# Nine chunk places in rotation for the expert weights, and VectorE's 32x32 turns in a triangular inversion

## The chip, the core and the metric

The kernel runs on one core of a Trainium2 chip. The metric is the time of the whole program on the device, in microseconds; lower is better. The profile gives the span from the first to the last instruction, which is a little shorter than that time. TensorE (PE in the profile) multiplies matrices, VectorE (DVE) and ScalarE (ACT) work on elements, and SyncE (SP) issues nearly all of the loads. "PEld" is the load of the stationary operand of a matmul.

## The reference, cut to what matters

A decoder block over 256 tokens of width 1024, in f32. It has three stages.

1. A mixer. Half of its heads are attention, the other half a gated delta rule over chunks of 64 tokens. For four heads and four chunks the delta rule solves a lower triangular system whose diagonal is one:

```
a_strict = where(strict, (k_beta @ k.T) * decay, 0)             # 64 x 64 for each head and chunk
uw = triangular_solve(a_strict + I, rhs, lower, unit_diagonal)  # rhs: v * beta | k_beta * exp(g)
```

2. Cross attention over 256 memory tokens.
3. A mixture of 32 experts, four for each token. Each expert has a gate and up matrix (1024 x 2048), a clamped SwiGLU and a down matrix (1024 x 1024). Whatever the routing is, the kernel reads all 32 experts' weights: 32 x 12 MiB.

## The kernel before

**Queues and buffers.** Each engine runs its own instruction list, and semaphores order them. Weights come in chunks of 128 x 4096 f32, 2 MiB, each a contiguous piece of its matrix. `ring` has six such places (`slot(0)` to `slot(5)`). `W_ORDER` names the 13 chunks of the first two stages; the n-th goes to slot n mod 6. SP issues one DMA for a chunk (L350, for experts L382) after it has waited for `slot_free`, which TensorE raises when the place's last matmul is done. TensorE waits for `slot_loaded`.

**The experts.** They are taken in 16 pairs with `PAIR_CHUNKS` = 12 chunks each: 0 to 3 are gate and up of the pair's first expert, 4 to 7 those of the second, 8 and 9 the first down matrix, 10 and 11 the second. `gate_up` (L1558) and `down` (L1585) are the matmuls that read chunks, `gather` (L1537) picks the tokens of the two experts of the next pair, and L1623 adds a pair's result to the tokens. Three more places lie in the `work` buffer (`extra`, numbers 6, 7 and 8), where data of the earlier stages is dead by then. For the first pair alone, chunks 6, 7 and 8 go into these; they are loaded in the order 0, 1, 2, 3, 6, 4, 7, 8, 5, 9, 10, 11. Place 6 may be written once ScalarE has the biases ready (`biases_ready`), places 7 and 8 after ScalarE has drained `x_pv1`, a step near the end of cross attention. All other chunks go round the six slots, `chunk_place` says where. TensorE and SP run pair 0 as straight code and the pairs 1 to 14 (SP: 1 to 15) in a loop with one pair in its body. Further passes over all experts exist for the case that one expert has more than 64 tokens; they are not entered with these inputs.

**The inversion.** The 64 x 64 systems are kept as eight matrices of 128 x 128, each with two systems on its diagonal. The inverse is built in six levels, each of which joins diagonal blocks two by two: `a_mat` masked to the level's blocks is `level_l` (`level_part`, L786 on VectorE). With the inverse so far as `inv` and its transpose as `inv_T`, a level is: `swap`n = level_l.T inv_T (TensorE, eight matmuls, L1244), ScalarE copies it out (L447), `solve_T`n = inv.T swap, which VectorE subtracts from inv_T (L890), and `solve`n, the same product the other way round, which VectorE subtracts from inv (L894). Level 0 needs no product: `inv` = 1 - level_l (L806), and `swap0` turns level_l on TensorE (against the identity), from which VectorE makes inv_T (L879). The blocks of `inv` are 2 wide after level 0 and 32 wide after level 4; level 5 makes inv_T alone.

**The order around it.** `EARLY`, `MIDDLE` and `LATE` are lists written by hand. In `MIDDLE` the levels stand between quarters of projections, such as `moba_v.0` (16 matmul records of 128 x 256, L1296 or L1300), so that TensorE has work while the others copy. Every named step writes one of four pairs of PSUM banks, and `take` waits until the pair's last content has been drained. Quarters use pair 3, the levels the pairs 0 and 1 in turn.

Of the kernel before, what the change touches and what calls it, by code (L numbers as in the profile page):

```python
# [20 lines left out]
ALU = mybir.AluOpType  # L21
# [20 lines left out]
PAIR_CHUNKS = 12  # L42
EPS = 1e-6
# [18 lines left out]
MIDDLE = ["swap0", "moba_v.0", "swap1", "moba_v.1", "solve_T1", "solve1", "moba_v.2", "swap2", "moba_v.3", "solve_T2",  # L62
# [34 lines left out]
def bass_hybrid_block(nc, x, mem, norm_mix_g, w_in, gdn_conv_w, gdn_A_log, gdn_dt_bias, gdn_norm_g,  # L97
                      moba_norm_g, w_out, norm_xattn_g, norm_mem_g, xattn_w_q, xattn_w_kv, xattn_w_o,
                      norm_ffn_g, router_w, router_b, w_gate_up, b_gate_up, w_down, b_down, final_norm_g, out):
    with ExitStack() as ctx:  # L100
# [196 lines left out]

        def slot(s):
            return ring[:, s * SLOT:(s + 1) * SLOT]
# [27 lines left out]
        def _(sp):  # L327
# [33 lines left out]
            def load_pair(i, before, first=False):  # L361


                gu = [w_gate_up[0, bass.ds(2 * i + k, 1)].rearrange("e (c p j) n -> p (e c) (j n)", p=P, j=2)
                      for k in range(2)]
                dn = [w_down[0, bass.ds(2 * i + k, 1)].rearrange("e (c p j) n -> p (e c) (j n)", p=P, j=4)
                      for k in range(2)]

                for c in (0, 1, 2, 3, 6, 4, 7, 8, 5, 9, 10, 11) if first else range(PAIR_CHUNKS):
                    dst, loaded, free, use = chunk_place(c, first)  # L370
                    if c < 8:
                        src = gu[c // 4][:, c % 4, :]
                    else:
                        src = dn[(c - 8) // 2][:, c % 2, :]
                    if free:
                        sp.wait_ge(S(free), 2 * before + use)
                    else:

                        sp.wait_ge(S("biases_ready"), 1)
                        if c > min(extra):  # L380
                            drained(sp, "x_pv1")
                    sp.dma_start(dst, src).then_inc(S(loaded), 16)  # L382

            load_pair(0, 0, first=True)
            with sp.Fori(1, PAIRS) as i:
                load_pair(i, i)
# [3 lines left out]
            with sp.If(most > SLOTS):  # L390
                with sp.Fori(1, PASSES) as r:
                    with sp.If(most > r * SLOTS):
                        with sp.Fori(0, PAIRS) as i:
                            load_pair(i, sp.snap(r * PAIRS + i))
# [41 lines left out]
        def _(act):  # L436
# [76 lines left out]
            for name in MIDDLE:  # L513
# [6 lines left out]
                elif name.startswith("swap") and name != "swap0":  # L520
# [124 lines left out]
        def _(v):  # L645
# [160 lines left out]
            nc.vector.tensor_tensor(inv, eye, level_l, ALU.subtract).then_inc(S("solved"), 1)  # L806
            drained(v, "tok_v")
# [372 lines left out]
        def _(pe):  # L1180
# [162 lines left out]
            for name in MIDDLE:  # L1343
# [201 lines left out]
            def chunk_landed(c, before, first):  # L1545
                place, loaded, free, use = chunk_place(c, first)
                pe.wait_ge(S(loaded), 32 * before + 16 * (use + 1))
                return place, free

            def gate_up(k, before, first):  # L1550
                for c in range(4):
                    place, free = chunk_landed(4 * k + c, before, first)
                    w = place.rearrange("p (k n) -> p k n", n=2 * D_MODEL)
# [6 lines left out]
                    if free:  # L1560
                        last.then_inc(S(free), 1)
# [13 lines left out]
            def down(k, n, before, first):  # L1575
# [4 lines left out]
                for c in range(2):  # L1580
                    place, free = chunk_landed(8 + 2 * k + c, before, first)
                    w = place.rearrange("p (k n) -> p k n", n=D_MODEL)
# [5 lines left out]
                    if free:  # L1588
                        last.then_inc(S(free), 1)
# [5 lines left out]
            def pair_of_experts(r, i, before, n, m, first=False, final=False):  # L1595
# [5 lines left out]
                gate_up(0, before, first)  # L1601
# [9 lines left out]
                gate_up(1, before, first)  # L1611
# [3 lines left out]
                down(0, n, before, first)  # L1615
                act_turned(1, m)
                down(1, m, before, first)
# [14 lines left out]
            def expert_pass(r, first=False):  # L1632
                pe.wait_ge(S("picked"), PAIRS * r + 1)
                gather(0, 0)
                gather(1, 0)
                drained(pe, "count")
                pe.wait_ge(S("count_ready"), 1)
                pe.wait_ge(S("biases_ready"), 1)
                if first:
                    pair_of_experts(r, 0, 0, 1, 2, first=True)  # L1640
                with pe.Fori(1 if first else 0, PAIRS - 1) as i:
                    pair_of_experts(r, i, pe.snap(r * PAIRS + i), pe.snap(r * E + 2 * i + 1),
                                    pe.snap(r * E + 2 * i + 2))
                i = PAIRS - 1
                pair_of_experts(r, i, pe.snap(r * PAIRS + i), pe.snap(r * E + 2 * i + 1), pe.snap(r * E + 2 * i + 2),
                                final=True)
# [3 lines left out]
            expert_pass(0, first=True)  # L1650
            most = pe.value_load(count_i[0:1, 0:1], min_val=0, max_val=SEQ)
            with pe.If(most > SLOTS):
                with pe.Fori(1, PASSES) as r:
                    with pe.If(most > r * SLOTS):
                        expert_pass(r)
# [24 lines left out]
```

## Time and profile before

| | us |
|---|---|
| median of three runs | 1262.95 (1260.44 to 1263.8) |
| the profiled execution, its own time | 1259.65 |
| its span | 1257.9 |
| TensorE busy with matmuls | 1127.2 (90%) |
| VectorE busy | 362.6 (29%) |
| ScalarE busy | 160.1 (13%) |
| bytes moved by DMA | 435.43 MB, 346 GB/s over the span |

How to read it: TensorE's share is that of a pipelined engine and counts records one after the other, so 90% doesn't say that it sets the end. The span falls into the two first stages (0 to about 324 us) and the experts (from there to 1239 us), with a short end. These two have to be read apart, in windows, together with the DMA rate.

### The profile page before, as it was taken

How to read it: one execution, taken by the hardware profiler on the slowest of the kernel's cores; microseconds unless marked ns; L12 is line 12 of the kernel's file. 1: busy time of each engine (PE TensorE's matmuls, PEld its weight loads, DVE VectorE, ACT ScalarE, POOL GpSimd, SP SyncE). 2: the span in 40 equal slices, each digit the busy share in tenths (PEclk: the TensorE clock that was granted, in tenths of full speed). 3: DMA queues.
4: the chain of work that ended last, by engine and by line, in shares of the span. 5: the costliest groups of instructions: out<-in, count | busy, mean ns of one | idle time of the engine just before them, and what ended most of it. 6: DMA issues, size and time to landing. Idle time of an engine off the chain costs nothing.

```text
span 1257.9 us, 15864 instructions
## 1 busy us (share of the span) xinstructions
PE 1127.2 (90%) x6688; PEld 556.9 (44%) x6688; DVE 362.6 (29%) x713; ACT 160.1 (13%) x241; POOL 5.5 (0%) x23
## 2 busy tenths in 40 slices
PE   7999998888899999898989898999989898989895
PEld 6889987475433333332423333333323232333331
DVE  5582234244321321221221312212122121221312
ACT  3431133243000000100000000000010000000001
POOL 1000000000000000000000000000000000000000
PEclk9999998998899999999999999999999999999998
DMA  9731221465588999999999999999999999999994
GB/s 336 268 134 68 67 68 67 110 261 207 219 356 359 427 429 427 429 429 428 429 427 429 429 428 429 427 430 428 428 429 427 430 428 428 430 427 430 428 428 188
DMA packets 45159, 435.43 MB, mean 346 GB/s; under 512 B 6581, under 2 KB 6666, under 8 KB 20458
## 3 DMA queue, kind: packets, MB, share of 16 engines
q1 hardware_dynamic: 42986, 433.16, 82.6%
q10 hardware_dynamic: 2144, 1.86, 0.7%
q8 instruction: 22, 0.36, 0.1%
q14 instruction: 7, 0.06, 0.0%
HBM read 433.95 MB, written 1.05 MB: 346 GB/s over the span
## 4 chain that ended last, share of the span: by engine, by line
PE 64%; DMA 27%; DVE 5%; ACT 2%; issue 1%; SPq 0%; ACTq 0%; DVEq 0%
PE ps L1558 28%; DMA ring<-in_w_down 25%; PE ps L1585 7%; PE ps L1623 5%; PE ps L1244 4%; PE ps L1200 4%; PE ps L1537 4%; PE ps L1300 3%; PE ps L1296 2%; PE ps L1182 2%; DVE work L1125 2%; PE ps L1429 1%; PE ps L1473 1%; DMA work<-in_b_down 1%; DMA ring<-in_w_in 1%
## 5 line engine op out<-in xcount | busy, mean ns | idle before, releaser
L1558 PE MATMUL ps<-ring,work 128*64 128x512 f32 x2016 | 445.4, 595 | 22.3 <-DMA ring<-in_w_gate_up 20.8
L1558 PEld LDWEIGHTS ps<-ring,work 128*64 128x64 f32 x2016 | 141.9, 137 | 302.2 <-issue 258.9
L1585 PE MATMUL ps<-ring,work 128*64 128x512 f32 x1008 | 229.1, 598 | 42.5 <-ACT work L623 23.6
L1585 PEld LDWEIGHTS ps<-ring,work 128*64 128x64 f32 x1008 | 68.3, 136 | 181.6 <-issue 113.4
L1102 DVE TENSOR_SCALAR work<-ps 128x512 f32<-128x512 f32 x32 | 21.9, 686 | 212.9 <-PE ps L1182 212.9
L621 ACT ACTIVATE work<-work 128x512 f32<-128x512 f32 x32 | 20.2, 630 | 488.7 <-DVE work L1102 488.7
L1125 DVE COPY work<-ps 128x1024 f32<-128x1024 f32 x16 | 19.6, 1224 | 217.6 <-PE ps L1591 217.6
L1623 PE MATMUL ps<-work 128*128 128x512 f32 x128 | 59.2, 605 | 21.1 <-DVE work L1125 21.1
L1117 DVE COPY work<-ps 128x512 f32<-128x512 f32 x16 | 11.1, 691 | 229.8 <-PE ps L1182 229.8
L1182 PE MATMUL ps<-small,work 128*128 128x128 f32 (+1 forms) x353 | 57.6, 297 | 13.6 <-DMA work<-in_gdn_conv_w 6.4
L623 ACT COPY work<-ps 128x512 f32<-128x512 f32 x32 | 18.7, 585 | 363.1 <-PE ps L1182 363.1
L1244 PE MATMUL ps<-work 128*128 128x128 f32 (+4 forms) x440 | 58.9, 286 | 6.1 <-ACT work L519 2.8
L1182 PEld LDWEIGHTS ps<-small,work 128*128 128x128 f32 (+1 forms) x353 | 44.2, 170 | 41.6 <-issue 39.8
L1200 PE MATMUL ps<-work,ring 128*128 128x256 f32 x256 | 58.7, 388 | 2.6 <-DMA ring<-in_w_in 2.2
L1244 PEld LDWEIGHTS ps<-work 128*128 128x128 f32 (+2 forms) x440 | 54.0, 187 | 11.4 <-issue 4.8
L1537 PEld LDWEIGHTS ps<-work 128*128 128x128 bf16 x1536 | 49.2, 100 | 10.9 <-issue 8.6
L1200 PEld LDWEIGHTS ps<-work,ring 128*128 128x128 f32 x256 | 49.1, 195 | 10.0 <-issue 3.4
L1537 PE MATMUL ps<-work 128*128 128x64 bf16 x1536 | 49.7, 196 | 2.3 <-DVE work L1065 2.3
L1130 DVE TENSOR_TENSOR work<-work,ps 128x1024 f32<-128x1024 f32 x32 | 39.1, 1221 | 42.3 <-PE ps L1623 42.3
L1623 PEld LDWEIGHTS ps<-work 128*128 128x128 f32 x128 | 23.0, 189 | 55.2 <-DVE work L1125 32.3
L1300 PE MATMUL ps<-ring,work 128*128 128x256 f32 x192 | 46.0, 395 | 0.0
L1300 PEld LDWEIGHTS ps<-ring,work 128*128 128x128 f32 x192 | 37.1, 198 | 5.7 <-issue 0.3
(209 smaller groups left out, 665.6 us busy)
## 6 DMA issues: line engine op xcount, KB each, us to landing
ring<-in_w_gate_up SPq DMA_DIRECT2D x126, 2048.0 KB, 24.8
ring<-in_w_down SPq DMA_DIRECT2D x63, 2048.0 KB, 22.9
ring<-in_w_in SPq DMA_DIRECT2D x7, 2048.0 KB, 16.0
ring<-in_xattn_w_kv SPq DMA_DIRECT2D x2, 2048.0 KB, 14.5
ring<-in_w_out SPq DMA_DIRECT2D x2, 2048.0 KB, 8.4
work<-in_w_gate_up SPq DMA_DIRECT2D x2, 2048.0 KB, 12.8
ring<-in_xattn_w_q SPq DMA_DIRECT2D x1, 2048.0 KB, 9.4
ring<-in_xattn_w_o SPq DMA_DIRECT2D x1, 2048.0 KB, 8.9
```

What stands on the lines that cost most here:

```text
L1102: nc.vector.tensor_scalar(gate_sb, bank(GATE_BANK[k]), LIMIT, None, ALU.min) \
L1125: nc.vector.tensor_copy(y_sb, ps[:, 512 * Y_BANK:512 * Y_BANK + 1024].rearrange("p (a b) -> p a b", b=512)).then_inc(S("y_ready"), 1)
L1130: nc.vector.tensor_tensor(x_sb[:, t, :], x_sb[:, t, :], ps[:, 512 * b:512 * b + 1024], ALU.add).then_inc(S("combined"), 1)
L1182: return nc.tensor.transpose(dst, src, ident[0:n_in, 0:n_in])
L1200: last = nc.tensor.matmul(pair(name)[:, SEQ * b:SEQ * b + SEQ], w[:, k, b * P:(b + 1) * P], moving[:, k, :], start=(k == 0), stop=(k == KB ...
L1244: return nc.tensor.matmul(dst, still, moving, start=True, stop=True)
L1296: last = nc.tensor.matmul(pair(name)[:, SEQ * q:SEQ * q + SEQ], w[:, k, q * P:(q + 1) * P], hT[:, k, :], start=(k == 0), stop=(k == KB - 1))
L1300: last = nc.tensor.matmul(halves(name)[:, t, c:c + 256], tokens[:, k, t * P:(t + 1) * P], w[:, k, c:c + 256], start=(k == 0), stop=(k == K ...
L1537: last = nc.tensor.matmul(dst[:, SLOTS * b:SLOTS * b + SLOTS], split[s][:, t, 2 * P * (b // 2) + b % 2:2 * P * (b // 2 + 1):2], pick[k][:, ...
L1558: last = nc.tensor.matmul(bank(b)[p], xg_T[k][:, kb, :], w[:, kk, 512 * q:512 * q + 512], start=(kb == 0), stop=False)
L1585: last = nc.tensor.matmul(bank(Y_BANK + y)[p], act_T[:, b, HALF * c:HALF * c + HALF], w[:, b, 512 * q:512 * q + 512], start=(c == 0 and b ...
L1623: last = nc.tensor.matmul(bank(b + q), g_T[:, q, P * t:P * t + P], y_sb[:, q, :], start=True, stop=True)
```

## The change

Two parts. First, the expert chunks of the first pass go round nine places, the six slots and the three in `work`, in the order `PLACES`, instead of six. 36 chunks, three pairs, are four turns of the nine places, so the loops of TensorE and SP now have three pairs in their body (four turns, pairs 1 to 12); pair 0 and the pairs 13 to 15 are straight code. The chunks are loaded in their order, 0 to 11. The first load of each place in `work` waits for both `biases_ready` and `x_pv1`.

Second, the turns in the inversion. `inv_T` of level 0 and `inv` after the levels 1 to 4 are made by VectorE with `transpose`, which turns each 32 x 32 block in its own place; since the blocks of these matrices are at most 32 wide, that is their transpose. `swap0` and `solve1` to `solve4` are gone, on TensorE and VectorE. `level_part(1)` comes before `tok_v` is scaled.

```diff
+PLACES = [1, 2, 3, 4, 5, 6, 7, 8, 0]
+TURN_PAIRS = 3
+TURN_USES = TURN_PAIRS * PAIR_CHUNKS // len(PLACES)
+TURNS = (PAIRS - 1 - TURN_PAIRS) // TURN_PAIRS
...
-MIDDLE = ["swap0", "moba_v.0", "swap1", "moba_v.1", "solve_T1", "solve1", "moba_v.2", "swap2", "moba_v.3", "solve_T2",
-          "solve2", "moba_q.0", "swap3", "moba_q.1", "solve_T3", "solve3", "moba_q.2", "swap4", "moba_q.3",
-          "solve_T4", "solve4", "moba_k.0", "moba_k.1", "swap5", "moba_k.2", "solve_T5", "moba_k.3", "u",
+MIDDLE = ["moba_v.0", "swap1", "moba_v.1", "solve_T1", "moba_v.2", "swap2", "moba_v.3", "solve_T2",
+          "moba_q.0", "swap3", "moba_q.1", "solve_T3", "moba_q.2", "swap4", "moba_q.3",
+          "solve_T4", "moba_k.0", "moba_k.1", "swap5", "moba_k.2", "solve_T5", "moba_k.3", "u",
           "w_T", "score0", "state0", "gdn_z.0", "v1", "inter1", "probs_T0", "state1", "gdn_z.1", "pv0",
...
-        FIRST_RING = PAIR_CHUNKS - len(extra)
-
-        def chunk_place(c, first):
-            if first and c in extra:
-                return extra[c], f"extra_loaded{c}", None, 0
-            if first:
-                n = PRE + c - sum(e < c for e in extra)
-            else:
-                n = PRE + FIRST_RING + c - PAIR_CHUNKS
-            return slot(n % RING), f"slot_loaded{n % RING}", f"slot_free{n % RING}", n // RING
+        def place(s):
+            return slot(s) if s < RING else extra[s]
+
+        def uses_before_experts(s):
+            return len(range(s, PRE, RING)) if s < RING else 0
+
+        def first_pass_chunk(i, c):
+
+            g = PAIR_CHUNKS * i + c
+            s = PLACES[g % len(PLACES)]
+            return s, uses_before_experts(s) + g // len(PLACES)
+
+        def later_pass_chunk(c):
+
+            s = c % RING
+            return s, uses_before_experts(s) + len(range(PLACES.index(s), PAIRS * PAIR_CHUNKS, len(PLACES))) + c // RING
...
-                for c in (0, 1, 2, 3, 6, 4, 7, 8, 5, 9, 10, 11) if first else range(PAIR_CHUNKS):
-                    dst, loaded, free, use = chunk_place(c, first)
+                for c in range(PAIR_CHUNKS):
+                    s, use = chunk(c)
                     if c < 8:
                         src = gu[c // 4][:, c % 4, :]
                     else:
                         src = dn[(c - 8) // 2][:, c % 2, :]
-                    if free:
-                        sp.wait_ge(S(free), 2 * before + use)
+                    if s >= RING and use == 0:
+
+                        sp.wait_ge(S("biases_ready"), 1)
+                        drained(sp, "x_pv1")
                     else:
-
-                        sp.wait_ge(S("biases_ready"), 1)
-                        if c > min(extra):
-                            drained(sp, "x_pv1")
-                    sp.dma_start(dst, src).then_inc(S(loaded), 16)
-
-            load_pair(0, 0, first=True)
-            with sp.Fori(1, PAIRS) as i:
-                load_pair(i, i)
+                        sp.wait_ge(S(f"slot_free{s}"), turned + use)
+                    dst = place(s)
+                    sp.dma_start(dst, src).then_inc(S(f"slot_loaded{s}"), 16)
+
+            load_pair(0, lambda c: first_pass_chunk(0, c), 0)
+            with sp.Fori(0, TURNS) as rev:
+                turned = sp.snap(rev * TURN_USES)
+                for q in range(1, TURN_PAIRS + 1):
+                    load_pair(rev * TURN_PAIRS + q, lambda c: first_pass_chunk(q, c), turned)
+            for i in range(PAIRS - TURN_PAIRS, PAIRS):
+                load_pair(i, lambda c: first_pass_chunk(i, c), 0)
...
             nc.vector.tensor_tensor(inv, eye, level_l, ALU.subtract).then_inc(S("solved"), 1)
+            v.wait_ge(S("solved"), 1)
+            nc.vector.transpose(flat(inv_T), flat(inv)).then_inc(S("inv_T_begun"), 1)
+            level_part(1)
             drained(v, "tok_v")
             nc.vector.tensor_tensor(tok_v, tok_v, spread(beta, P), ALU.mult).then_inc(S("vb_ready"), 1)
...
-                if name == "swap0":
-                    filled(v, name)
-                    drain_done(nc.vector.tensor_tensor(inv_T, eye, blocks(name), ALU.subtract), name)
-                    v.wait_ge(S("solved"), 1)
-                    level_part(1)
-                    drained(v, name)
-                elif name.startswith("swap"):
+                if name.startswith("swap"):
 
                     if n + 1 < LEVELS:
                         filled(v, name)
                         level_part(n + 1)
                 elif name.startswith("solve_T"):
                     filled(v, name)
+                    if n == 1:
+                        v.wait_ge(S("inv_T_begun"), 1)
                     drain_done(nc.vector.tensor_tensor(inv_T, inv_T, blocks(name), ALU.subtract), name)
                     drained(v, name)
-                elif name.startswith("solve"):
-                    filled(v, name)
-                    drain_done(nc.vector.tensor_tensor(inv, inv, blocks(name), ALU.subtract), name)
-                    drained(v, name)
+                    if n + 1 < LEVELS:
+                        nc.vector.transpose(flat(inv), flat(inv_T)).then_inc(S("inv_turned"), 1)
...
-                elif name == "swap0":
-                    pe.wait_ge(S("level_ready"), 1)
-                    eight(name, lambda b, dst: mm(dst, level_l[:, b, :], ident))
                 elif name.startswith("swap"):
                     pe.wait_ge(S("level_ready"), n + 1)
-                    drained(pe, "swap0" if n == 1 else f"solve_T{n - 1}")
+                    if n == 1:
+                        pe.wait_ge(S("inv_T_begun"), 1)
+                    else:
+                        drained(pe, f"solve_T{n - 1}")
                     eight(name, lambda b, dst: mm(dst, level_l[:, b, :], inv_T[:, b, :]))
                 elif name.startswith("solve_T"):
                     drained(pe, f"swap{n}")
                     if n == 1:
                         pe.wait_ge(S("solved"), 1)
                     else:
-                        drained(pe, f"solve{n - 1}")
+                        pe.wait_ge(S("inv_turned"), n - 1)
                     eight(name, lambda b, dst: mm(dst, inv[:, b, :], swap[:, b, :]))
-                elif name.startswith("solve"):
-                    eight(name, lambda b, dst: mm(dst, swap[:, b, :], inv[:, b, :]))
...
-            def chunk_landed(c, before, first):
-                place, loaded, free, use = chunk_place(c, first)
-                pe.wait_ge(S(loaded), 32 * before + 16 * (use + 1))
-                return place, free
-
-            def gate_up(k, before, first):
+            def chunk_landed(s, use, turned16):
+                pe.wait_ge(S(f"slot_loaded{s}"), turned16 + 16 * (use + 1))
+                return place(s)
+
+            def gate_up(k, chunk, turned16):
                 for c in range(4):
-                    place, free = chunk_landed(4 * k + c, before, first)
-                    w = place.rearrange("p (k n) -> p k n", n=2 * D_MODEL)
+                    s, use = chunk(4 * k + c)
+                    w = chunk_landed(s, use, turned16).rearrange("p (k n) -> p k n", n=2 * D_MODEL)
...
+            def first_pass():
+                begin_pass(0)
                 drained(pe, "count")
                 pe.wait_ge(S("count_ready"), 1)
                 pe.wait_ge(S("biases_ready"), 1)
-                if first:
-                    pair_of_experts(r, 0, 0, 1, 2, first=True)
-                with pe.Fori(1 if first else 0, PAIRS - 1) as i:
+                pair_of_experts(0, 0, 0, 1, 2, lambda c: first_pass_chunk(0, c), 0)
+                with pe.Fori(0, TURNS) as rev:
+                    turned16 = pe.snap(rev * (16 * TURN_USES))
+                    for q in range(1, TURN_PAIRS + 1):
+                        i = pe.snap(rev * TURN_PAIRS + q)
+                        pair_of_experts(0, i, i, pe.snap(2 * i + 1), pe.snap(2 * i + 2),
+                                        lambda c: first_pass_chunk(q, c), turned16)
+                for i in range(PAIRS - TURN_PAIRS, PAIRS):
+                    pair_of_experts(0, i, i, 2 * i + 1, 2 * i + 2, lambda c: first_pass_chunk(i, c), 0,
+                                    final=(i == PAIRS - 1))
```

## Rows read from the trace of the kernel before

**Rows 1.** The page: busy time of the engines, and GB/s in 40 equal slices.
```profile
PE 1127.2 (90%) x6688; PEld 556.9 (44%) x6688; DVE 362.6 (29%) x713; ACT 160.1 (13%) x241; POOL 5.5 (0%) x23
...
GB/s 336 268 134 68 67 68 67 110 261 207 219 356 359 427 429 427 429 429 428 429 427 429 429 428 429 427 430 428 428 429 427 430 428 428 430 427 430 428 428 188
```

**Rows 2.** Windows of one pair each; the last two columns are DMA share and GB/s.
```profile
651.19:709.91 58.72, 52.64 (x320) 19.85 (x321) 13.37 (x27) 3.71 (x5) 0.00 (x0) 1.00 1.01 428
324.26:379.00 54.74, 52.02 (x322) 20.48 (x321) 13.82 (x30) 3.71 (x5) 0.00 (x0) 0.99 0.84 343
```

**Rows 3.** Chain that ended last: last down chunk of pair 3 and of pair 14.
```profile
533.73 3.65 PE ps L1585 x16
...
1179.74 3.65 PE ps L1585 x16
```

**Rows 4.** Timeline of the end: the last down chunk and the last instruction.
```profile
1238.80 3.65 PE L1585 MATMUL ps<-ring,work 128*64 128x512 f32 x16 [1.23 <-DMA ring<-in_w_down]
...
1253.55 1.28 DVE L1176 SCALAR_TENSOR_TENSOR work<-work,small 128x1024 f32<-128x1024 f32 x1
```

**Rows 5.** SP's own timeline, the issues of chunks around the start of the experts.
```profile
294.30 0.33 SPq L382 DMA_DIRECT2D work<-in_w_gate_up  x1
...
303.18 0.33 SPq L382 DMA_DIRECT2D ring<-in_w_gate_up  x1
...
328.23 0.33 SPq L382 DMA_DIRECT2D ring<-in_w_down  x1
...
346.70 0.33 SPq L382 DMA_DIRECT2D ring<-in_w_gate_up  x1
...
362.48 0.33 SPq L382 DMA_DIRECT2D ring<-in_w_gate_up  x1
...
382.82 0.33 SPq L382 DMA_DIRECT2D ring<-in_w_gate_up  x1
```

**Rows 6.** Windows of 5 us: the stream's start and the two dips of its rate.
```profile
330.00:335.00 5.00, 5.00 (x26) 1.65 (x24) 0.00 (x0) 0.00 (x0) 0.00 (x0) 1.00 0.94 380
...
360.00:365.00 5.00, 4.32 (x24) 1.85 (x22) 0.00 (x0) 1.73 (x2) 0.00 (x0) 1.00 0.37 85
...
380.00:385.00 5.00, 5.00 (x26) 1.69 (x24) 0.00 (x0) 0.00 (x0) 0.00 (x0) 1.00 0.31 69
```

**Rows 7.** TensorE's timeline of pair 0 and the start of pair 1.
```profile
324.26 14.23 PE L1558 MATMUL ps<-ring,work 128*64 128x512 f32 x64
...
363.89 7.09 PE L1585 MATMUL ps<-ring,work 128*64 128x512 f32 x32 [0.68 <-ACT work L623]
...
379.00 13.95 PE L1558 MATMUL ps<-ring,work 128*64 128x512 f32 x64
```

**Rows 8.** Timeline of the inversion's head and its first full level.
```profile
87.34 1.95 PE L1244 MATMUL ps<-small,work 128*128 128x128 f32 x16
87.54 1.01 ACT L447 COPY work<-ps 128x1024 f32<-128x1024 f32 x1 [0.36 <-PE ps L1182]
...
88.94 1.23 DVE L806 TENSOR_TENSOR work<-small,work 128x1024 f32<-128x1024 f32 x1
...
92.35 1.22 DVE L786 TENSOR_TENSOR work<-work,small 128x1024 f32<-128x1024 f32 x1
...
93.62 2.05 PE L1244 MATMUL ps<-work 128*128 128x128 f32 x16 [0.88 <-DVE work L786]
...
95.51 3.62 PE L1300 MATMUL ps<-ring,work 128*128 128x256 f32 x16
...
98.96 3.73 PE L1244 MATMUL ps<-work 128*128 128x128 f32 x32
```

**Rows 9.** VectorE by line and shape: one input of 1024 columns; two of 2048.
```profile
L662 DVE TENSOR_SCALAR work<-work,small 128x1024 f32<-128x1024 f32 x6 | 4.5, 753 | 0.2
...
L767 DVE TENSOR_TENSOR work<-work 128x2048 f32<-128x2048 f32 x1 | 2.3, 2292 | 0.0
```

**Rows 10.** DMA queues, an instruction queue: packets, MB, share of 16 engines.
```profile
q8 instruction: 22, 0.36, 0.1%
```

More of the change, by code:

```diff
@@ L296, in spread, with flat @@
             return v.unsqueeze(2).to_broadcast([v.shape[0], v.shape[1], n])
+        def flat(v):
+            return v.rearrange("p a b -> p (a b)")
         def slot(s):
@@ L359, in _, with load_pair @@
                             .then_inc(S(f"mem_loaded{t}"), 16)
-            def load_pair(i, before, first=False):
+            def load_pair(i, chunk, turned):
                 gu = [w_gate_up[0, bass.ds(2 * i + k, 1)].rearrange("e (c p j) n -> p (e c) (j n)", p=P, j=2)
@@ L393, in _ @@
                         with sp.Fori(0, PAIRS) as i:
-                            load_pair(i, sp.snap(r * PAIRS + i))
+                            load_pair(i, later_pass_chunk, sp.snap((r - 1) * 2 * PAIRS + 2 * i))
             for t in range(TILES):
@@ L519, in _ @@
                     drain_done(nc.scalar.copy(m_pT, halves(name)[:, :, 0:384]), name)
-                elif name.startswith("swap") and name != "swap0":
+                elif name.startswith("swap"):
                     evacuate(name, swap, blocks(name))
@@ L1559, in gate_up @@
                                                     start=(kb == 0), stop=False)
-                    if free:
-                        last.then_inc(S(free), 1)
+                    last.then_inc(S(f"slot_free{s}"), 1)
                 for q, (b, p) in enumerate(((GATE_BANK[k], low), (GATE_BANK[k], high),
@@ L1573, in act_turned, with down @@
                 last.then_inc(S("act_T_filled"), 1)
-            def down(k, n, before, first):
+            def down(k, n, chunk, turned16):
                 pe.wait_ge(S("act_T_ready"), n)
@@ L1580, in down @@
                 for c in range(2):
-                    place, free = chunk_landed(8 + 2 * k + c, before, first)
-                    w = place.rearrange("p (k n) -> p k n", n=D_MODEL)
+                    s, use = chunk(8 + 2 * k + c)
+                    w = chunk_landed(s, use, turned16).rearrange("p (k n) -> p k n", n=D_MODEL)
                     for b in range(4):
@@ L1587, in down @@
                                                     start=(c == 0 and b == 0), stop=False)
-                    if free:
-                        last.then_inc(S(free), 1)
+                    last.then_inc(S(f"slot_free{s}"), 1)
                 for q, (y, p) in enumerate(places):
@@ L1593, in down, with pair_of_experts @@
                 last.then_inc(S("down_filled"), 1)
-            def pair_of_experts(r, i, before, n, m, first=False, final=False):
+            def pair_of_experts(r, i, before, n, m, chunk, turned16, final=False):
                 pe.wait_ge(S("gathered"), E * r + 2 * i + 1)
@@ L1600, in pair_of_experts @@
                 pe.wait_ge(S("combined"), 2 * before + 1)
-                gate_up(0, before, first)
+                gate_up(0, chunk, turned16)
                 pe.wait_ge(S("gated_picked"), PAIRS * r + i + 1)
@@ L1610, in pair_of_experts @@
                 pe.wait_ge(S("gathered"), E * r + 2 * i + 2)
-                gate_up(1, before, first)
+                gate_up(1, chunk, turned16)
                 act_turned(0, n)
                 pe.wait_ge(S("gated_T_ready"), before + 1)
-                down(0, n, before, first)
+                down(0, n, chunk, turned16)
                 act_turned(1, m)
-                down(1, m, before, first)
+                down(1, m, chunk, turned16)
                 pe.wait_ge(S("y_ready"), before + 2)
@@ L1630, in pair_of_experts, with begin_pass @@
                     gather(1, 0)
-            def expert_pass(r, first=False):
+            def begin_pass(r):
                 pe.wait_ge(S("picked"), PAIRS * r + 1)
@@ L1638, in expert_pass, with later_pass @@
                 pe.wait_ge(S("biases_ready"), 1)
-                if first:
-                    pair_of_experts(r, 0, 0, 1, 2, first=True)
-                with pe.Fori(1 if first else 0, PAIRS - 1) as i:
+                pair_of_experts(0, 0, 0, 1, 2, lambda c: first_pass_chunk(0, c), 0)
[8 more added lines that the diff above has]
+                                    final=(i == PAIRS - 1))
+            def later_pass(r):
+                begin_pass(r)
+                done = pe.snap((r - 1) * PAIRS)
+                with pe.Fori(0, PAIRS - 1) as i:
                     pair_of_experts(r, i, pe.snap(r * PAIRS + i), pe.snap(r * E + 2 * i + 1),
-                                    pe.snap(r * E + 2 * i + 2))
+                                    pe.snap(r * E + 2 * i + 2), later_pass_chunk, pe.snap(done * 32 + 32 * i))
                 i = PAIRS - 1
                 pair_of_experts(r, i, pe.snap(r * PAIRS + i), pe.snap(r * E + 2 * i + 1), pe.snap(r * E + 2 * i + 2),
-                                final=True)
+                                later_pass_chunk, pe.snap(done * 32 + 32 * i), final=True)
             pe.sem_inc(S("act_T_filled"), 1)
-            expert_pass(0, first=True)
+            first_pass()
             most = pe.value_load(count_i[0:1, 0:1], min_val=0, max_val=SEQ)
@@ L1654, in _ @@
                     with pe.If(most > r * SLOTS):
-                        expert_pass(r)
+                        later_pass(r)
 _INS = ["x", "mem", "norm_mix_g", "w_in", "gdn_conv_w", "gdn_A_log", "gdn_dt_bias", "gdn_norm_g", "moba_norm_g",
```

## The prediction

> **What bounds the kernel now.** I read the page's slices first. From slice 14 (409 us) on the loads run at 427 to 430 GB/s without a break, while in the slices before they move less [rows 1]. So there are two regimes. The windows of one pair say what each costs: a late pair takes 58.72 us at a DMA share of 1.01; pair 0, for which nine chunks lay ready, takes 54.74 us [rows 2]. TensorE alone would need 54.74 us for a pair, the loads need 58.72 us, 4.893 us for each of 12 chunks. The chain shows how exact this is: from the last down chunk of pair 3 to that of pair 14 it is 646.01 us, 11 pairs of 58.73 us [rows 3]. The last chunk of all is multiplied at 1238.80 us, at once after its landing, and 19.1 us of adding, norm and store follow to the end of the span, 1257.9 us [rows 4]. Nothing that TensorE does after 500 us sets the end. It is: the time at which the stream of 183 chunks (192 less the nine loaded ahead) begins, plus 183 x 4.893 = 895.4 us, plus what the stream idles, plus the tail.
>
> **Where the stream begins and idles.** With nine places full, SP waits for TensorE's first chunk: the experts' matmuls begin at 324.26 us [rows 7] and SP issues the tenth chunk at 328.23 us [rows 5]. The reader is to see in the next issues that only six slots come round. Six chunks go out up to 346.70 us; the next is issued at 362.48 us, since it waits for slot 1, which holds chunk 9, a down chunk of pair 0. While TensorE works on the chunks in places 6, 7 and 8 it frees nothing. Three issues follow from 362.48 us on, then again none until 382.82 us, when the first chunk of pair 1 is done [rows 5]. The windows over these stretches show 85 and 69 GB/s [rows 6].
>
> I rebuild it as a queue: a chunk starts 1.76 us after its issue if the queue is empty (from the 380 GB/s of the window up to 335 us [rows 6]), else behind the one ahead, and takes 4.893 us. The stream starts at 329.99 us. Six chunks are done at 359.35, the seventh starts at 364.24: 4.9 us idle. The eighth starts 0.35 us late, the ninth ends at 379.27 and the tenth starts at 384.58: 5.3 us idle. Together 10.5 us. Check: 329.99 + 895.4 + 10.5 = 1235.9 us; TensorE takes the last chunk at 1238.80, so 2.9 us lie between end of service and use. I keep these as they are.
>
> **Part one, nine places.** Chunk 9 now goes to the place of chunk 0, and every later one nine behind. The frees of pair 0, counted from its matmul rows [rows 7], come at 327.9, 331.3, 334.8, 338.2, 343.0, 346.4, 349.9, 353.4, 358.7, 362.1, 367.4 and 370.9 us, the next at 382.5 us with pair 1. Twelve chunks keep the queue busy until 329.99 + 12 x 4.893 = 388.7 us, and the thirteenth can start at 384.6 (its issue at 382.82 us and 1.76). That is the tightest place, with 4.1 us in hand; each later pair adds 58.72 - 54.74 = 4.0 us. So the 10.5 us go to zero: **-10.5 us**. After that the nine places give nothing, as six already keep the stream full.
>
> The loading order also moves. Chunks 5, 6 and 7 now wait for `x_pv1`, before that chunk 6 did not, and chunk 8 stands behind them on SP. In the clock of before: three issues at 294.30 and one at 303.18 us [rows 5], four chunks in a row, done at 296.1 + 4 x 4.893 = 315.6 us. TensorE starts at 324.26 and wants chunk 5 only at 343. Cost nothing; were the cover gone, one chunk, 4.9 us.
>
> In the steady state SP has about eight chunks out instead of five. No row shows that a longer queue changes the rate: nothing for it.
>
> **Part two, the turns.** Through the levels TensorE has no idle time but 0.9 us; the levels and the quarters follow each other without a gap, so a removed matmul is time. A block of eight is 16 records, 1.95 us alone; `solve_T1` and `solve1` together are 32 records, 3.73 us [rows 8]. Each of `solve1` to `solve4` gives 1.78 us: 7.1 us. VectorE does a turn in place of the subtraction L894. The turn must be done before the next `solve_T`, which comes a quarter (3.62), a swap (1.95) and another quarter later [rows 8]; with the subtraction (1.22 us) ahead of it, some 5 us are in hand. ScalarE's copy of `swap`n lies under a quarter as before.
>
> At the head less is gained. Without `swap0` (87.34 us), `moba_v.0` waits until ScalarE has copied `tok_v` (87.54 + 1.01 us) and starts at 88.7 instead of 89.1; it would be done at 92.2. `swap1` waits for `level_part(1)`, before at 92.35 us, followed by the matmul at 93.62 [rows 8]. Now VectorE does L806 at 88.94, the turn from 90.20 and `level_part(1)` after it; scaling `tok_v` is behind these. The trace has no such turn. Its cost for 128 x 1024 f32 is bounded by the nearest rows: 0.75 us for one input from SBUF at the same size, 2.29 us for two inputs of twice the size [rows 9]. I take 1.22, as nearly all rows of 1024 columns have [rows 8]. Then `level_part(1)` ends at 92.56 and `swap1` starts at 92.6: **-1.0 us**; with the bounds -1.4 and 0. This is the only place where the turn's length counts.
>
> The Trainium skill (VectorE: DVE Perf Modes, section The three transpose paths) gives 311 ns for a turn of 128 x 128 bf16; eight of these would be 2.5 us, an estimate from that page, and by it the head would gain nothing and the sum come out 1.0 us higher. No row here shows a turn.
>
> So the front is shorter by 8.1 us. Does that arrive at 324 us? After the levels everything is released by TensorE, VectorE or ScalarE, or by loads that SP and ScalarE issue after one of them; nothing in the chain there is tied to a fixed time. **-8.1 us**, bounds 7.1 and 8.5. The stream then starts 8.1 us earlier.
>
> **Part three, what the loops cost.** A pair is 320 + 321 records on TensorE [rows 2]. Four more bodies are now straight code (one body before and one in the loop, now four and three). An instruction queue moved 0.36 MB in 22 packets, 16.4 KB each [rows 10]; 2 x 6688 records of TensorE [rows 1] less 13 repeated pairs of 641 are 5043, so 71 bytes for each record, waits included. A loop's body fetched once fits these numbers; fetched each time there would be 0.59 MB more. Four more bodies are 0.18 MB, 11 packets: at 429 GB/s 0.4 us of the stream. I take **+0.5 us**. If one DMA engine carried them all, at 0.9 us for each (0.1% of 16 spans over 22 packets) it would be 10 us. Against that: the straight last pair, three packets, took from 1179.74 to 1238.80, only 0.3 us more than the 58.73 of the others [rows 3, 4].
>
> **Sum.** 1257.9 - 10.5 - 8.1 + 0.5 = 1239.8 us of span. The profiled execution's own time lies 1.75 us above its span: 1241.5. The median of the runs shown is 3.3 us above that execution, so I forecast 1244.5 us. What a measurement of this kernel can't tell from no change is about 0.3%, 4 us.
>
> **The rivals.**
> (a) Both parts pay as above: 1244.5 us, own range 1239 to 1250 (turn at its bounds, gap 9 to 11.5 us, up to 5 us of code loads). Chance 0.74.
> (b) Only the queue pays; the front's 8 us are lost to a wait behind it. For: the front has many waits of VectorE and ScalarE. Against: the chain there holds only short ones. 1252.6 us. Chance 0.07.
> (c) Only the front pays: the stream still idles, because SP's order or a late release of a place keeps it from using nine. For: each wait on SP holds all loads behind it. Against: the counted frees. 1255.0 us. Chance 0.07.
> (d) Slower: TensorE's loop body no longer stays loaded and is fetched each turn. That body is 3 x 641 records or 137 KB, while rows show only 46 KB held. Three repeats and the four more bodies are 36 packets; on one DMA engine 36 x 0.9 = 33 us that every chunk waits for, so 1277 us with the gains taken off. It decides from 20 packets on; spread over the engines it is 1.4 us and nothing. As stalls of TensorE alone it is hidden: to be the bound, TensorE would have to lose 1223.9 (end of the last chunk then) - 1184.2 (316.2 + 15 pairs of 54.74 + 46.9 for the last, as pair 0 [rows 7]) = 40 us first. Chance 0.08. The Trainium skill (Runtime: NRT & Kernel Launch, section Instruction fetch mechanics) says that a taken branch out of the fetched window forces a load of the target before execution goes on; by that rule the stall exists, and the trace of before shows no such stall at its loop's end.
> (e) No gain within 0.3%, both parts failing: 0.04.
>
> The range reaches over (a), (b) and (c): 1238 to 1255. Faster 0.90, same 0.03, slower 0.07.
>
> **What the profile after would show.** The first expert matmul at 316 us; SP's issues following the frees without the holes of 16 and 12 us; windows of 5 us from 325 to 375 us at 425 GB/s or more; the slices full from slice 11 on; TensorE at 54.7 us for a pair until pair 4 or 5 and at 58.7 us after it; issue to landing of a gate chunk near 39 us instead of 25; the last down chunk at 1220 us; 16 records in place of 32 in four levels, and turns of about 1.2 us. I am wrong if pairs take more than 58.7 us (code loads, or a longer queue slows the stream), if the instruction queue shows 60 packets or more, or if the experts start later than 318 us.

## The result and the profile after

The changed kernel takes 1250.87 us (median of 5 runs, 1246.79 to 1252.57), the kernel before 1261.31 us in the same comparison: ratio 0.991, 95% interval 0.9886 to 0.9936. It is faster by 10.4 us where 18 were forecast. The time lies inside the forecast's range (1238 to 1255), but 0.9 us outside the likeliest case's own range (1239 to 1250). The profiled execution took 1252.57 us, its span is 1250.8 us.

The page of the kernel after, its GB/s in 40 slices and its instruction queue, against [rows 1] and [rows 10]:

```profile
GB/s 338 270 80 122 70 74 61 110 202 268 269 427 426 428 429 427 428 422 428 427 427 428 425 428 427 427 427 428 424 427 427 428 429 427 427 428 429 428 427 125
...
q8 instruction: 61, 1.00, 0.3%
```

Two things are to be seen. The stream is full from slice 11 on, where before it was full from slice 13 on: the holes are closed. And the instruction queue moved 61 packets instead of 22; the prediction had named 60 or more as a sign against it. Its two other signs came too: the experts start at 319.08 us, later than 318, and some pairs take more than 58.7 us. The last down chunk starts at 1231.64 us, not at 1220, and a gate chunk lands 34 to 35 us after its issue (medians of the page), not 39.

SP's timeline and the chain of waits of the kernel after, against [rows 5] and [rows 3]: the first refill, the loop's first jump back, and the last down chunks of pairs 6, 8, 9 and 11:

```profile
322.88 7.20 SPq L394 DMA_DIRECT2D ring<-in_w_down  x3
```

```profile
537.82 6.74 issue
544.55 15.65 PE ps L1568 x64
...
698.37 3.65 PE ps L1594 x16
...
817.37 3.65 PE ps L1594 x16
...
876.10 3.65 PE ps L1594 x16
...
995.10 3.65 PE ps L1594 x16
```

At the end of pair 3, TensorE stands still for 6.7 us with nothing to wait for, and its next 64 records take 15.65 us instead of 13.95 (why is said in the last section). Pair 9, with no turn's end in it, takes 58.73 us as before; pairs 7 and 8 take 119.00 us together and 10 and 11 again 119.00, where two pairs took 117.46 before. Windows of the kernel after, columns as in [rows 2]: pair 0, the standstill, pair 9, and pairs 7 and 8:

```profile
319.15:373.66 54.51, 51.80 (x323) 20.45 (x322) 13.75 (x30) 3.71 (x5) 0.00 (x0) 1.00 0.92 386
...
538.00:545.00 7.00, 0.45 (x2) 0.30 (x4) 0.00 (x0) 0.00 (x0) 0.00 (x0) 0.73 1.02 414
817.37:876.10 58.73, 52.57 (x320) 19.72 (x320) 13.36 (x27) 3.72 (x5) 0.00 (x0) 1.00 1.01 428
698.37:817.37 119.00, 106.35 (x640) 41.57 (x640) 26.74 (x54) 7.43 (x10) 0.00 (x0) 0.97 1.01 427
```

The loads go on during the standstill (414 GB/s), so it isn't waited for by itself; over the turn of pairs 7 to 9 the stream still loses 119.00 - 117.46 = 1.5 us. The end, timeline of TensorE, against [rows 4]:

```profile
1231.64 3.65 PE L1594 MATMUL ps<-ring,work 128*64 128x512 f32 x16 [1.03 <-DMA ring<-in_w_down]
```

The last down chunk still waits for its load and starts at 1231.64 us. From the experts' first matmul (319.08 us) to it are 912.56 us; before they were 1238.80 - 324.26 = 914.54. Of the 10.5 us of holes only 2.0 arrive. I call this length the stream's length below; it doesn't depend on when the front ends.

The head of the inversion, a timeline of all engines after, against [rows 8]:

```profile
93.41 3.72 PE L1313 MATMUL ps<-ring,work 128*128 128x256 f32 x16 [1.10 <-ACT work L463]
93.75 1.23 DVE L822 TENSOR_TENSOR work<-small,work 128x1024 f32<-128x1024 f32 x1
95.00 1.25 DVE L824 STREAM_TRANSPOSE work<-work 128x1024 f32<-128x1024 f32 x1
96.17 1.18 DVE L802 TENSOR_TENSOR work<-work,small 128x1024 f32<-128x1024 f32 x1
...
97.41 2.05 PE L1257 MATMUL ps<-work 128*128 128x128 f32 x16 [0.28 <-DVE work L802]
```

The turn takes 1.25 us (1.22 taken), `moba_v.0` waits 1.1 us for ScalarE's copy of `tok_v`, and `swap1` waits 0.28 us for `level_part(1)`. It all stands 4.8 us later than in the profile before, which has its cause ahead of the change: the first 64 records of a projection took 17.10 us here and 14.05 before. The repetition below shows that it is no part of the change.

### The profile page after: what moved, and what is told of

Its sections match the earlier page's. It is cut to its first block, busy times and chain, and to the rows that moved or that the text cites. A ratio compares the mean times of both kernels' runs of the same rounds, so it can differ in the third digit from the quotient of the medians.

```text
span 1250.8 us, 15537 instructions
## 1 busy us (share of the span) xinstructions
PE 1123.2 (90%) x6608; PEld 557.4 (45%) x6608; DVE 362.9 (29%) x713; ACT 160.2 (13%) x241; POOL 5.5 (0%) x23
## 4 chain that ended last, share of the span: by engine, by line
PE 65%; DMA 24%; DVE 5%; issue 3%; ACT 2%; SPq 0%; ACTq 0%; DVEq 0%
PE ps L1568 25%; DMA ring<-in_w_down 20%; PE ps L1594 11%; PE ps L1631 5%; PE ps L1213 4%; PE ps L1548 4%; PE ps L1257 4%; DMA work<-in_w_down 3%; PE ps L1313 3%; PE ps L1195 2%; PE ps L1309 2%; DVE work L1138 2%; PE ps L1440 1%; PE ps L1484 1%; DMA work<-in_b_down 1%
## 5 line engine op out<-in xcount | busy, mean ns | idle before, releaser
L1568 PE MATMUL ps<-ring,work 128*64 128x512 f32 x1360 | 306.2, 605 | 26.4 <-issue 21.4
L1568 PEld LDWEIGHTS ps<-ring,work 128*64 128x64 f32 x1360 | 97.0, 140 | 217.2 <-issue 206.9
L1594 PE MATMUL ps<-ring,work 128*64 128x512 f32 x704 | 158.7, 597 | 23.1 <-ACT work L639 12.3
L1568 PE MATMUL ps<-work 128*64 128x512 f32 x688 | 153.0, 594 | 5.6 <-DMA work<-in_w_gate_up 5.6
L1594 PEld LDWEIGHTS ps<-ring,work 128*64 128x64 f32 x704 | 50.4, 137 | 115.9 <-issue 87.4
L1568 PEld LDWEIGHTS ps<-work 128*64 128x64 f32 x688 | 48.0, 137 | 101.0 <-issue 89.0
L1594 PE MATMUL ps<-work 128*64 128x512 f32 x320 | 72.0, 595 | 8.6 <-ACT work L639 4.1
L1213 PE MATMUL ps<-work,ring 128*128 128x256 f32 x256 | 62.3, 405 | 2.3 <-DMA ring<-in_w_in 1.8
L1257 PE MATMUL ps<-work 128*128 128x128 f32 (+4 forms) x376 | 54.1, 296 | 5.5 <-ACT work L535 2.8
L1213 PEld LDWEIGHTS ps<-work,ring 128*128 128x128 f32 x256 | 51.8, 205 | 10.7 <-issue 3.0
L1257 PEld LDWEIGHTS ps<-work 128*128 128x128 f32 (+2 forms) x376 | 48.9, 191 | 11.3 <-issue 5.1
```

What stands on the lines that cost most here:

```text
L1213: last = nc.tensor.matmul(pair(name)[:, SEQ * b:SEQ * b + SEQ], w[:, k, b * P:(b + 1) * P], moving[:, k, :], start=(k == 0), stop=(k == KB ...
L1257: return nc.tensor.matmul(dst, still, moving, start=True, stop=True)
L1568: last = nc.tensor.matmul(bank(b)[p], xg_T[k][:, kb, :], w[:, kk, 512 * q:512 * q + 512], start=(kb == 0), stop=False)
L1594: last = nc.tensor.matmul(bank(Y_BANK + y)[p], act_T[:, b, HALF * c:HALF * c + HALF], w[:, b, 512 * q:512 * q + 512], start=(c == 0 and b ...
```

## The experiments

Theory: nine places close the holes in full, and the loop body of three pairs takes the gain back, since it doesn't stay loaded: each turn loads its code again, and these loads slow the stream. Rivals: the longer queue of nine places slows the stream by itself; the front's gain was smaller than its matmuls; TensorE's standstills cost the time, not the loads.

**The changed kernel again**, unchanged.

> The changed kernel once more, as the yardstick of this chip. Both theories expect what was measured: about 10 us under the kernel before (ratio 0.991), three stalls of TensorE of about 7 us at the ends of the loop's turns, and 61 packets on the instruction queue. If the late first stage of the profiled execution (the first 64 records of a projection took 17.1 us against 14.1) was chance, the experts' first matmul comes here at 314 to 317 us instead of 319; if it belongs to the change, again at 319.

Measured: 1248.75 us against 1261.27 us, ratio 0.9917 (0.9894 to 0.994). Three standstills of 6.7, 6.1 and 6.5 us, 61 packets, and the experts' first matmul at 314.87 us. The first projection, timeline of TensorE:

```profile
12.73 15.64 PE L1213 MATMUL ps<-work,ring 128*128 128x256 f32 x64 [1.59 <-DMA ring<-in_w_in]
```

15.64 us, with the same instructions as 17.10: the late first stage is no part of the change. It also varies in kernels with the old front (17.07 us in the kernel with six places and three pairs in the body, below). The granted clock goes with it: the traces have it on record at full from 10.8 us on where the projection took 14.05 us, from 16.0 us where it took 15.64 and from 19.0 us where it took 17.10. In the straight kernel below (15.74 us) it stood at the lower of its two levels (1.2 GHz, 0.50 of full) from 13.8 to 17.2 us. Behind the projection it was lower too, 0.58 over the stretch from 31.3 to 39.4 us against 0.79 before. So the starts of single profiles differ by up to 5 us, and the parts are better read from medians and from the stream's length.

**The turns alone.** The kernel before with the second part only:

```diff
             nc.vector.tensor_tensor(inv, eye, level_l, ALU.subtract).then_inc(S("solved"), 1)
+            v.wait_ge(S("solved"), 1)
+            nc.vector.transpose(flat(inv_T), flat(inv)).then_inc(S("inv_T_begun"), 1)
+            level_part(1)
...
-                elif name.startswith("solve"):
-                    eight(name, lambda b, dst: mm(dst, swap[:, b, :], inv[:, b, :]))
```

> The kernel before with the turns on VectorE alone, six places. If the second part is worth what its removed matmuls say: 8 us less than before (ratio 0.9935), the experts' first matmul at 316 us, holes in the stream as before. If the part is worth less, because a wait behind it takes it back: 0 to 4 us less, and the experts' start at 320 us or later.

Measured: 1254.0 us, ratio 0.9941 (0.9924 to 0.9958), 7.3 us under 1261.27. The experts' first matmul comes at 316.81 us, 7.45 us earlier than in the profile before; 8.1 was forecast. The interval of the ratio reaches from 5.3 to 9.6 us, so the two can't be told apart. The stream's length is 914.17 us, with the holes in it. The front pays.

**The nine places alone.** The changed kernel with the inversion of before (`MIDDLE`, `swap0` and `solve1` to `solve4` put back on both engines).

> The changed kernel with the inversion of before: nine places and three pairs in a loop body. Theory of the code loads: of the 10.5 us of holes that are closed, 8 us are given back in the stream, so only 2 to 3 us less than before (ratio 0.998), with 61 packets on the instruction queue and late pairs with a turn's end in them 1.5 us longer than 58.73. Rival, that the queue pays in full and the front is at fault: 10 us less (ratio 0.992).

Measured: 1258.81 us over 12 runs, ratio 0.998 (0.997 to 0.999), 2.5 us under before; 59 packets, stream's length 911.37 us. 7.3 and 2.5 make 9.8 us, about what the whole change has (10.4). The first part is the one that lost its gain.

**Six places, but three pairs in TensorE's loop body.** The kernel before with this alone:

```diff
-                with pe.Fori(1 if first else 0, PAIRS - 1) as i:
-                    pair_of_experts(r, i, pe.snap(r * PAIRS + i), pe.snap(r * E + 2 * i + 1),
-                                    pe.snap(r * E + 2 * i + 2))
+                    with pe.Fori(0, 4) as rev:
+                        for q in range(1, 4):
+                            i = pe.snap(rev * 3 + q)
+                            pair_of_experts(r, i, i, pe.snap(2 * i + 1), pe.snap(2 * i + 2))
+                    for i in range(PAIRS - 3, PAIRS - 1):
+                        pair_of_experts(r, i, i, 2 * i + 1, 2 * i + 2)
```

> The kernel before, with six places, its old inversion and SP's loop of one pair; only TensorE's loop body has three pairs (four turns, then three straight). Theory of the code loads: about 60 packets on the instruction queue, three stalls of 7 us, and 6 to 9 us slower than before (ratio 1.006), the stalls hidden or not. Rival, that the longer DMA queue of the nine places slows the stream: this kernel takes the time of before, within 2 us, since its queue is no longer.

Measured: 1270.13 us, ratio 1.0064 (1.0048 to 1.0081), 8.9 us slower. No place, no load and no product differs from the kernel before. Its instruction queue and one of its three standstills (page and chain of waits):

```profile
q8 instruction: 59, 0.97, 0.3%
```

```profile
728.61 5.05 issue
```

So the longer body alone costs about what the nine places lost, and the longer queue isn't needed for it. The loads and the standstills are still together in this kernel.

**No loop at all.** The changed kernel with TensorE's pairs 1 to 15 as straight code, to part the loads from the standstills:

```diff
-                with pe.Fori(0, TURNS) as rev:
-                    turned16 = pe.snap(rev * (16 * TURN_USES))
-                    for q in range(1, TURN_PAIRS + 1):
...
+                for i in range(1, PAIRS):
```

> The changed kernel with TensorE's 16 pairs all as straight code; SP keeps its loop of three pairs. The same number of pairs' code is loaded (16 bodies of about 2.8 packets, near 60 packets in all), but nothing is jumped back over. If the loads themselves cost the stream its 8 us: the time of the changed kernel, within 2 us, with no stall of TensorE in it. If the stalls of 7 us after the jumps cost it: 6 to 8 us under the changed kernel (ratio 0.986 to the kernel before).

Measured: 1249.86 us, ratio 0.9895 (0.9876 to 0.9913) against 1262.14 us of its own comparison; the changed kernel had 0.9917. 54 packets, no standstill, stream's length 909.72 us. So the loads alone cost most of it: with nothing jumped back over, the stream is still 5 us longer than it could be. It is 2.5 us shorter than the 912.2 us (mean of two profiles) of the changed kernel. By the ratios the kernel is 2.8 us faster than that one, a little more than the 2 us that I allowed, with intervals that overlap, and far from the rival's 6 to 8 us. Seven packets fewer would be 1.4 us of it. The third standstill costs nothing: from pair 8's last down chunk to the last of all, with that standstill in between, the two profiles of the changed kernel take 414.27 and 414.38 us and the straight kernel 414.30. Whether the first two have the rest stays open.

The straight kernel shows best how the loads cost time, since nothing else disturbs its late pairs. Last down chunks of pairs 9, 10 and 11, chain of waits:

```profile
870.15 3.65 PE ps L1594 x16
930.40 3.65 PE ps L1594 x16
989.16 3.65 PE ps L1594 x16
```

Pair 10 takes 60.25 us, pair 11 58.76. From pair 6 to pair 14 the pairs take 58.76, 60.28, 58.74, 58.72, 60.25, 58.76, 58.73, 60.27 and 58.74 us: most take the 58.7 us of the kernel before, although nine places are in use, and every third takes 1.5 us more. Three pairs are some eight packets of code, so 1.5 us are 0.19 us for each. The changed kernel's 119.00 us against 117.46 are the same 1.5 us.

**Nine places only as long as they are needed.** Pairs 0 to 3 straight with nine places, then the six slots and a loop body of one pair:

```diff
+HEAD = 4
+TURN_PAIRS = 1
+TURN_USES = 2
+TURNS = 11
+SIX = [4, 5, 0, 1, 2, 3]
+
+
+def place_of(g):
+    return PLACES[g % 9] if g < 48 else SIX[(g - 48) % 6]
```

> The changed kernel with nine places only up to chunk 47, the end of pair 3, and the six slots from pair 4 on: pairs 0 to 3 straight, a loop body of one pair for the pairs 4 to 14, pair 15 straight. The queue model (4.893 us for a chunk, TensorE at 54.74 us for a pair) gives no hole with this. Theory of the code loads: 6 bodies of straight or once loaded code instead of 16, near 31 packets, 2 us of the stream instead of 8, so 6 us under the changed kernel (ratio 0.987). Rival, that nine places are needed throughout: holes come back after pair 4, and the time is at or over the changed kernel's.

Measured: 1241.86 us, ratio 0.9847 (0.9826 to 0.9867), 20.3 us under before; 29 packets, no standstill, stream's length 905.54 us.

**Eight places in rotation, a body of two pairs.** The ninth place is used once:

```diff
+HEAD = 1
+TURN_PAIRS = 2
+TURN_USES = 3
+TURNS = 7
+EIGHT = [1, 2, 3, 4, 5, 6, 8, 0]
+
+
+def place_of(g):
+    return 7 if g == 7 else EIGHT[(g if g < 7 else g - 1) % 8]
```

> The changed kernel with eight places in rotation (24 chunks, two pairs, are three turns of them) and the ninth used once, for chunk 7 of pair 0; pair 0 straight, a loop body of two pairs in seven turns, pair 15 straight. The queue model gives 0.9 us of holes. If a body of two pairs, some 91 KB, stays loaded as that of one pair does: near 28 packets, no stalls, 6 us under the changed kernel (ratio 0.987). If it is loaded again each turn: near 60 packets, six stalls of 7 us, the time of the changed kernel or more.

Measured: 1241.8 us, ratio 0.9839 (0.9819 to 0.9859), 20.3 us under before; stream's length 905.36 us. Its instruction queue on the page, and a window of two pairs, from the last down chunk of pair 11 to that of pair 13, with a jump back in it:

```profile
q8 instruction: 24, 0.39, 0.1%
```

```profile
985.18:1102.65 117.47, 105.28 (x640) 39.97 (x641) 26.73 (x54) 7.43 (x10) 0.00 (x0) 1.00 1.01 428
```

117.47 us over a jump back, against 119.00 us in the changed kernel: a body of two pairs (1282 records, an estimated 91 KB at the prediction's 71 bytes each) stays loaded, one of three (137 KB) doesn't. Both last kernels are faster than the changed one by some 9 us; between them nothing can be told.

The stream's length against the packets of the whole program, one profile each:

| kernel | packets | stream's length, us |
|---|---|---|
| before, with its 10.5 us of holes taken off | 22 | 904.0 |
| eight places, body of two, 0.9 us of holes taken off | 24 | 904.5 |
| nine, then six, body of one | 29 | 905.5 |
| nine places, straight | 54 | 909.7 |
| nine places alone, body of three, old inversion | 59 | 911.4 |
| changed kernel, two profiles | 61 | 912.6 and 911.9 |

From 22 to 61 packets it grows by 8.2 us, 0.21 us for each packet; the straight kernel alone gives (909.7 - 904.0) / 32 = 0.18 us.

## Why the prediction was right, and where it missed

**The number: inside the range, in part by luck.** The range went up to 1255 us for the rivals (b), a front that doesn't pay, and (c), nine places that don't. The measured 1250.87 lies nearer to (b)'s 1252.6 than to the forecast's 1244.5, but the runs refute both: the front pays and the holes close. What filled the gap was the mechanism of rival (d), a body that doesn't stay loaded, at a quarter of the price that the prediction had put on it (8.2 us, not 33).

**What bounds it: right.** The sum "start of the stream + 183 chunk times + holes + tail" (without holes 5.7 + 895.4 + 2.9 = 904.0 us from the experts' first matmul to the last chunk) describes the profiles of the table once the packets have their price (the six-place kernel with three pairs in its body isn't in it, since its last expert's down matrix waited for ScalarE).

**The holes: right.** The first refill is issued at 322.88 us and slices 11 and 12 run at 427 and 426 GB/s. The kernels with few packets show the whole 10.5 us: 914.54 - 905.36 = 9.2 us, and 0.9 of holes and 0.4 for two packets are what is missing. That the longer queue costs nothing holds as well: most late pairs of the straight kernel take 58.7 us with nine places. One reading was loose: the 1.76 us from issue to start don't follow from the 380 GB/s of the window from 330 to 335 us alone, which gives 2.3 us; they come out if the 49 GB/s of the 5 us ahead of it are counted too.

**The turns: right.** 7.3 us alone (5.3 to 9.6), forecast 8.1; the 0.8 us between them are within the noise. The turn takes 1.25 us. The 2.5 us that I estimated from a figure of the Trainium skill (VectorE: DVE Perf Modes, section The three transpose paths) for bf16 is not what this turn of f32 shows.

**The loading order: right.** Nothing in the profiles waits for chunks 5 to 8.

**The code loads: the term that was mis-sized.** The prediction took +0.5 us: "Four more bodies are 0.18 MB, 11 packets: at 429 GB/s 0.4 us of the stream". Both factors failed. The number of packets was 39 and not 11, since the body of three pairs isn't kept over a jump back: 16 pairs' code is loaded instead of three, 3.0 packets for each of 13 more. This was rival (d)'s mechanism, with a count of 36, which I gave 0.08. And a packet costs 0.21 us, not the 0.04 us of its 16.4 KB at 429 GB/s, nor the 0.9 us of one engine that holds up every chunk. 39 x 0.21 = 8.2 us, 7.7 more than forecast: 18.1 - 7.7 = 10.4 us, as measured, though the agreement to 0.1 us is chance with intervals of 2 us to either side. I had used the 0.3 us of the last pair as evidence against a dear packet. In the straight kernel two of three pairs show next to nothing and the third 1.5 us, so one pair with three packets could decide nothing.

**The standstills: right that they are hidden.** They take 19 us together, and the slower records behind them 6.6 us more (15.65, 16.62 and 16.19 instead of 13.95), of an estimated 40 us that TensorE could lose before it is the bound. The rule of the Trainium skill (Runtime: NRT & Kernel Launch, section Instruction fetch mechanics), that a taken branch out of the window waits for its target's load, is borne out by the body of three pairs, 5.9 to 6.7 us at each of three jumps, 5.1 to 5.5 with the old inversion. The same section states 128 KiB (131 KB) for TensorE's instruction memory. The bodies fall on either side of it: 91 KB stays, 137 KB doesn't. The section also speaks of only two lines of 16 KiB and doesn't say whether that holds for TensorE; by it the bodies of 46 and 91 KB would be loaded again at every turn, and 22 and 24 packets show that they aren't.

## What to carry to other kernels

When loads set the end, price a longer loop body in instruction packets: count its records, see whether the body is still kept over the jump (the packets on the instruction queue tell), and add their cost, here 1.5 us for eight of them, to the stream and not to the engine that stalls. A deeper prefetch pays only while the consumer is ahead, here for the first four of 16 pairs; after that the fewest places whose rotation gives a short loop body do the same. Compare a period that can't move with the front (here from the experts' first matmul to the last chunk), since single profiles differ by some microseconds in when the clock comes up.

## What the runs showed of the hardware that was not expected

A 16.4 KB packet of instructions takes 0.2 us from a saturated stream of 429 GB/s, five times its share by bytes. The traces show how the cost comes about. In the straight kernel the records of single instruction packets repeat with a period of eight. From 587 us on they last 1.07, 1.08, 1.06, 1.10, 1.11, 1.09, 1.03 and 1.01 us, then 1.07, 1.07, 1.06, 1.10, 1.10, 1.09, 1.03 and 1.02, and so on. The stream loses its 1.5 us once in about as many packets. And at its end half of the DMA engines' time is idle in the changed kernel where the kernel before has all of it in use. The windows reach from 10 to 5 us ahead of the last chunk's first matmul, after and then before:

```profile
1221.64:1226.64 5.00, 4.55 (x22) 1.74 (x22) 0.00 (x0) 0.32 (x1) 0.00 (x0) 1.00 0.50 213
1228.80:1233.80 5.00, 4.44 (x22) 1.63 (x22) 0.00 (x0) 0.52 (x1) 0.00 (x0) 1.00 1.03 436
```

The same window shows a share of 0.62 in the straight kernel (54 packets), 1.01 in the kernel with nine and then six places (29) and 1.00 in that with eight (24). All this fits instruction packets that go round eight of the 16 DMA engines. Each holds up one engine; a chunk lands with its slowest part, so the landings move back when the round comes to an engine for the next time, and at the end eight engines have work left while the others are done. 39 packets are 4.9 rounds, 7.5 us at 1.54 us each, of the 8.2 measured. That it is eight engines is my inference, as the traces don't name the engine of a packet. Why an engine loses 1.5 us where its packet lasts 1.1 stays open.

TensorE stood still from 537.82 us on, and its granted clock fell from full to the lower of its two levels (1.2 GHz) from 541.2 to 548.0 us; the mean over the window from 538 to 545 us is the 0.73 above. That is why the next 64 records took 15.65 us instead of 13.95.
